# The second token tile's transposes move behind the high products of the first tile's second half unit, and TensorE's two layer loops are written out

## The chip, the cores and the metric

The kernel runs on one core of one Trainium2 chip. The metric is the device time of one execution in microseconds, as the median of several runs. Weights and inputs come from the device's memory (HBM), and 340 MB of them pass through the core's DMA queues in one execution.

## The reference, cut to what matters

Two transformer blocks of two layers each run one after the other on 256 tokens of width 1024. In the first block a layer is:

```
h = rmsnorm(x, g_pre_mix);  proj = h @ w_in;  four kinds of attention on slices of proj
x = x + rmsnorm(mix @ w_out, g_post_mix)
h = rmsnorm(x, g_pre_mlp);  m = square(relu(h @ w_up)) @ w_down;  x = x + rmsnorm(m, g_post_mlp)
x = x + sigmoid(x @ w_ple_gate) * (p_i @ w_ple_proj)
```

and in the second block:

```
z = x @ w_in + b_in;  dilated window attention and retention on slices of z;  gates;  mix = merged @ w_out
x = layer_norm(ALPHA * x + mix)
ffn = (silu(x @ w_gate) * (x @ w_up)) @ w_down;  x = layer_norm(ALPHA * x + ffn)
```

Everything is float32. The change touches the places where a new stage begins with a product of the freshly updated `x` and a weight matrix.

## The kernel before, in words

**Splitting.** Each float32 product is made of three products of shorter operands: high weights times high activations (`whi`, `XH`), high weights times low activations (`whi`, `XL`), and low weights times high activations (`wlo`, `XH`). The first two are called the high products here, the third the low products. ScalarE (ACT) makes the high part by a copy into the shorter type, and VectorE (DVE) makes the low part by a subtraction.

**Units.** A weight unit is 512 rows (four blocks of 128) by 512 columns, 1 MB. SyncE (SP) loads units into four slots of `raw`. ACT turns unit u into `whi[u % 2]` (line 1090, tile `whi`) and DVE turns it into `wlo[u % 2]` (line 1544, or in two halves at line 1556). The 256 tokens are two tiles m = 0 and m = 1 of 128. A half unit is a unit's work for one token tile: eight high products (lines 596 and 597, in turn), then four low products (line 602). A chunk of 512 output columns takes two units k = 0 and k = 1, so four half units, called m0k0, m0k1, m1k0 and m1k1 below.

**Turning.** Products contract over the 1024 features, so `x` must be transposed first. TensorE (PE) turns four 128 x 128 blocks into one of two banks of `T` (line 634), ACT copies the bank to `XH` (line 1090, times a gain vector in the first block's norms, then as four instructions of 128 columns), and DVE makes `XL` from it (line 1585 with the gain, line 1582 without), which also frees the bank. A token tile takes two banks, so eight transposes.

**A stage's beginning.** `first_chunk` is used at five places in a pair of layers, so at ten in the program: the first projection of a layer of the first block, its MLP (`U_MLP`), its PLE gate (`U_PLE1 + 1`), the first projection of a layer of the second block, and its feed-forward (`V_FFN`). Tile 0 has been turned before it, inside the last half unit of the stage ahead (`turn_ahead` as the `between` of `last_pair`). Then come m0k0, the turn of tile 1 (`row_turn`, which waits for `s_x`, set when DVE has written the new rows of `X` for tile 1), m0k1, m1k0 and m1k1. The rows of `X` come at line 1748 in the first block's norms and at line 2129 in the second block's.

**What sets the order.** Every engine's instructions are written out by hand in its own block, and each engine takes them strictly in that order. Semaphores (`s_hi`: `whi` ready, `s_lo`: `wlo` ready, `s_used`: unit consumed, `s_t`: bank turned, `s_thi`: `XH` ready, `s_tfree`: `XL` ready and bank free, `s_x` and `s_xh`: rows of `X` ready) tie them together. At the MLP's and the PLE gate's beginning ACT makes `whi` of unit k = 1 only after the square root that tile 1's norm needs, and DVE makes `wlo` of k = 1 between the new rows of `X` and tile 1's `XL`:

```
root(0, L, 4, 2, 1, 1)                    # ACT: square root of tile 1's norm
hi(0, L, 0, U_MLP + 1)                    # ACT: whi of unit k = 1
row_hi(0, L, T_N2, 1, pre[:, 1, L])       # ACT: XH of tile 1
...
add_normed(2, 1)                          # DVE: rows of X, tile 1
lo(0, L, 0, U_MLP + 1)                    # DVE: wlo of unit k = 1
row_los(0, L, T_N2, 1, pre[:, 1, L])      # DVE: XL of tile 1
```

At the feed-forward's beginning (`V_FFN`) and at a layer's beginning `whi` of k = 1 is ahead of that square root, or there is no norm. At the beginning of the program, and of layer 1 of the first block, ACT also squares `X` after tile 1's `XH`, for the norm's factor, and only then makes `whi` of unit 2.

**Layer loops.** ACT, DVE and GpSimd have their layers written out. TensorE and SyncE run each block's two layers in a hardware loop (`Fori`), so on TensorE the value that a semaphore is waited for is worked out from the loop's register by a register instruction.

## Time and profile before

| | |
|---|---|
| runs | 1994.34, 2001.11, 2001.44 us, median 2001.11 |
| the profiled execution's own time | 1996.49 us |
| its span, from first to last instruction | 1994.7 us |
| TensorE matmuls, busy | 1905.3 us, 96% of the span, 9135 instructions |
| VectorE, busy | 1172.4 us, 59% |
| ScalarE, busy | 887.9 us, 45% |
| mean granted TensorE clock | 0.976 of full speed |
| moved by DMA | 340.25 MB, 171 GB/s |

The span is what the rows' times count in. The execution's own time is 1.8 us more than it. An engine's busy time is the union of its instructions. PEld is TensorE's loading of weights, which runs beside its matmuls. Matmuls overlap in these rows: one of 512 columns lasts 0.39 us from start to end, and the next starts some 0.23 us after it.

### The profile page before, as it was taken

The page shows a single profiled execution, that of the slowest core. Times are in us where ns is not written, and L with a number is a line of the kernel's source. Part 1 is how long each engine was busy: PE and PEld are TensorE (multiplying, and loading weights), DVE is VectorE, ACT ScalarE, POOL GpSimd, SP SyncE. Part 2 cuts the span into 40 slices and gives each one's busy share as a digit, 9 for nine tenths or more (in the row PEclk, how much of TensorE's full clock was granted, in tenths as well). Part 3 has the DMA queues.
Part 4 walks back from the last instruction along what each step waited for, and adds up shares of the span by engine and source line. Part 5 has one row for each costly group of instructions (what it writes and reads, how often), then busy time and mean ns, then how long its engine had stood idle before and what let it go on. Part 6 is the DMA issues. An engine that isn't in the chain of part 4 may idle for free.

```text
span 1994.7 us, 25098 instructions
## 1 busy us (share of the span) xinstructions
PE 1905.3 (96%) x9135; PEld 1564.7 (78%) x9135; DVE 1172.4 (59%) x1372; ACT 887.9 (45%) x1071; POOL 82.3 (4%) x97
## 2 busy tenths in 40 slices
PE   7988999999899999999999989998999999989997
PEld 6777888778678887888877778886888877778885
DVE  5775555667765456556566565445556566574445
ACT  5544444555344445444345334443344355434442
POOL 5300000022100000000000000000000000000000
PEclk9989999999799999999999999999999999999998
DMA  7404555553755555664455644555663455645553
GB/s 260 141 15 154 189 183 166 177 190 113 86 190 195 182 174 181 216 213 124 143 189 173 224 152 160 186 184 190 213 215 122 147 185 191 209 149 164 186 186 106
DMA packets 194402, 340.25 MB, mean 171 GB/s; under 512 B 9338, under 2 KB 59418, under 8 KB 194316
## 3 DMA queue, kind: packets, MB, share of 16 engines
q1 hardware_dynamic: 189072, 327.76, 50.0%
q0 software_dynamic: 5120, 11.15, 3.1%
q8 instruction: 60, 0.98, 0.2%
q10 hardware_dynamic: 123, 0.14, 0.0%
q14 instruction: 27, 0.21, 0.0%
HBM read 333.24 MB, written 5.77 MB: 170 GB/s over the span
## 4 chain that ended last, share of the span: by engine, by line
PE 83%; DVE 8%; ACT 3%; DVEq 3%; issue 2%; DMA 1%; SPq 0%; ACTq 0%
PE G L580 18%; PE G L581 18%; PE G L585 18%; PE T L634 5%; PE A L580 4%; PE A L581 4%; PE A L585 4%; PE G L602 2%; PE G L596 2%; PE G L597 2%; DVE wlo L1544 2%; ACT whi L1090 2%; PE T L684 1%; PE A L694 1%; ACT arena L1090 1%
## 5 line engine op out<-in xcount | busy, mean ns | idle before, releaser
L1544 DVE TENSOR_TENSOR wlo<-raw,whi 128x2048 fp32r<-128x2048 f32 (+2 forms) x316 | 666.7, 2111 | 617.9 <-ACT whi L1090 617.4
L1090 ACT ACTIVATE whi<-raw 128x2048 fp32r<-128x2048 f32 (+3 forms) x320 | 566.0, 1769 | 647.1 <-PE G L585 523.8
L580 PE MATMUL G<-whi,XH 128*128 128x512 f32 (+1 forms) x1408 | 560.8, 398 | 8.3 <-DVE XL L1568 6.6
L581 PE MATMUL G<-whi,XL 128*128 128x512 f32 (+1 forms) x1408 | 550.3, 391 | 0.0
L585 PE MATMUL G<-wlo,XH 128*128 128x512 f32 (+1 forms) x1408 | 346.2, 388 | 0.0
L580 PEld LDWEIGHTS G<-whi,XH 128*128 128x128 f32 x1408 | 266.7, 189 | 64.8 <-issue 8.4
L581 PEld LDWEIGHTS G<-whi,XL 128*128 128x128 f32 x1408 | 266.7, 189 | 54.1 <-issue 1.9
L585 PEld LDWEIGHTS G<-wlo,XH 128*128 128x128 f32 x1408 | 263.9, 188 | 53.6
L634 PE MATMUL T<-ident,arena 128*128 128x128 f32 x812 | 120.7, 289 | 25.5 <-ACT arena L1090 18.1
L634 PEld LDWEIGHTS T<-ident,arena 128*128 128x128 f32 x812 | 99.3, 148 | 45.3 <-ACT arena L1090 15.3
L1090 ACT ACTIVATE arena<-T 128x512 f32<-128x512 f32 (+2 forms) x92 | 46.2, 550 | 151.2 <-PE T L634 150.9
L596 PE MATMUL G<-whi,XH 128*128 128x512 f32 x192 | 77.6, 404 | 7.9 <-ACT whi L1090 6.4
L580 PE MATMUL G<-whi,MH 128*128 128x512 f32 x216 | 84.4, 391 | 0.0
L581 PE MATMUL G<-whi,ML 128*128 128x512 f32 x216 | 84.1, 389 | 0.0
L597 PE MATMUL G<-whi,XL 128*128 128x512 f32 x192 | 76.6, 399 | 0.0
L580 PE MATMUL A<-whi,MH 128*128 128x512 f32 x192 | 74.7, 389 | 0.0
L581 PE MATMUL A<-whi,ML 128*128 128x512 f32 x192 | 74.7, 389 | 0.0
L580 PE MATMUL A<-whi,XH 128*128 128x512 f32 (+1 forms) x160 | 62.2, 390 | 0.0
L581 PE MATMUL A<-whi,XL 128*128 128x512 f32 (+1 forms) x160 | 60.4, 379 | 0.0
L1090 ACT ACT_TABLE_LOAD x40 | 51.3, 1283 | 9.3 <-PE T L634 8.6
L585 PE MATMUL G<-wlo,MH 128*128 128x512 f32 x216 | 55.1, 389 | 0.0
L602 PE MATMUL G<-wlo,XH 128*128 128x512 f32 x192 | 54.3, 405 | 0.7 <-DVE wlo L1544 0.5
(225 smaller groups left out, 2066.7 us busy)
## 6 DMA issues: line engine op xcount, KB each, us to landing
raw<-in_w_in SPq DMA_DIRECT2D x112, 1024.0 KB, 6.7
raw<-in_w_mlp_up SPq DMA_DIRECT2D x32, 1024.0 KB, 5.4
raw<-in_w_mlp_down SPq DMA_DIRECT2D x32, 1024.0 KB, 5.0
raw<-in_w_ffn_gate SPq DMA_DIRECT2D x44, 512.0 KB, 4.0
raw<-in_w_ffn_up SPq DMA_DIRECT2D x44, 512.0 KB, 5.0
raw<-in_w_ffn_down SPq DMA_DIRECT2D x44, 512.0 KB, 3.3
raw<-in_w_out SPq DMA_DIRECT2D x16, 1024.0 KB, 5.0
raw<-in_w_ret_proj SPq DMA_DIRECT2D x16, 1024.0 KB, 5.1
```

Of the source, the lines that this page charges most:

```text
L580: nc.tensor.matmul(dst(m), hx[:, k0 + k, rows], hi[:, k, :], start=first and k == 0, stop=False)
L581: nc.tensor.matmul(dst(m), lx[:, k0 + k, rows], hi[:, k, :], start=False, stop=False)
L585: mm = nc.tensor.matmul(dst(m), hx[:, k0 + k, m * P:(m + 1) * P], lo[:, k, :], start=False, stop=last and k == kb - 1)
L596: nc.tensor.matmul(dst(m), hx[:, k0 + k, rows], hi[:, k, :], start=first and k == 0, stop=False)
L597: nc.tensor.matmul(dst(m), lx[:, k0 + k, rows], hi[:, k, :], start=False, stop=False)
L602: mm = nc.tensor.matmul(dst(m), hx[:, k0 + k, rows], lo[:, k, :], start=False, stop=last and k == kb - 1)
L634: tr = nc.tensor.transpose(T[:, t % 2, n * P:(n + 1) * P], src, ident[:])
L684: mm = nc.tensor.matmul(heads_out(q)[:, h * HD:(h + 1) * HD], PT2[m][:, h, kt, g * P:(g + 1) * P], ZV[:, kt, (g * HG + 2 * x + h) * HD:][: ...
L694: mm = nc.tensor.matmul(A[:, q % 2, u * HD:(u + 1) * HD], PT[:, q % 2, kt, u * P:(u + 1) * P], Z[:, kt, col:col + HD], start=kt == 0, stop ...
L1090: return nc.scalar.activation(out_, in_, func, **kw)
L1544: tt(wlo[:, c % PARTS, 0:n], raw[:, slot, 0:n], whi[:, c % PARTS, 0:n].bitcast(F32), ALU.subtract).then_inc(s_lo.sem, 1)
```

## The change

`row_turn` for tile 1 is no longer issued ahead of m0k1. It goes into m0k1 as its `between`, so between that half unit's eight high products and its four low products. And both layer loops of TensorE become Python loops, so that its instructions for the two layers stand one behind the other in the program. The loops inside a layer (over the MLP's and the feed-forward's column groups) stay hardware loops. No other engine's code is changed.

```diff
                 for m in range(TILES):
                     for k in range(2):
-                        if (m, k) == (0, 1):
-                            row_turn(blk, L, t, 1, s_x, x)
                         pe.wait_ge(s_tfree.sem, s_tfree.at(blk, L, t + 2 * m + k + 1))
-                        half_unit(blk, L, m, c + k, XH, XL, UK * k, UK, bank_pair(group), k == 0, k == 1)
+                        half_unit(blk, L, m, c + k, XH, XL, UK * k, UK, bank_pair(group), k == 0, k == 1,
+                                  between=(lambda: row_turn(blk, L, t, 1, s_x, x)) if (m, k) == (0, 1) else None)
...
-            with pe.Fori(0, DEPTH) as L:
+            for L in range(DEPTH):
 
                 first_chunk(0, L, 0, 0, 0)
...
-            with pe.Fori(0, DEPTH) as L:
+            for L in range(DEPTH):
                 def w_in_chunk(i, c, u):
```

On TensorE, at the beginning of the first block's MLP, the turn of tile 1 (`T<-ident,X`) stands before the change between m0k0's low products and m0k1's high products:

```order
L602 MATMUL A<-wlo,XH 128x512 [waits s_lo]
L602 MATMUL A<-wlo,XH 128x512 x3
L634 MATMUL T<-ident,X 128x128 [waits s_tfree,s_x]
L634 MATMUL T<-ident,X 128x128 x3
L632 REGISTER_ALU [waits s_x]
L634 MATMUL T<-ident,X 128x128 [waits s_tfree]
L634 MATMUL T<-ident,X 128x128 x3
L596 MATMUL A<-whi,XH 128x512 [waits s_hi,s_tfree]
L597 MATMUL A<-whi,XL 128x512
```

and with the change, at the same place, the last high products of m0k1 are ahead of it and its low products behind it:

```order
L596 MATMUL A<-whi,XH 128x512
L597 MATMUL A<-whi,XL 128x512
L634 MATMUL T<-ident,X 128x128 [waits s_tfree,s_x]
L634 MATMUL T<-ident,X 128x128 x3
L634 MATMUL T<-ident,X 128x128 [waits s_tfree,s_x]
L634 MATMUL T<-ident,X 128x128 x3
L602 MATMUL A<-wlo,XH 128x512 [waits s_lo]
L602 MATMUL A<-wlo,XH 128x512 x3
L596 MATMUL A<-whi,XH 128x512 [waits s_hi,s_tfree]
L597 MATMUL A<-whi,XL 128x512
```

The transposes have moved past eight matmuls and past the wait for `whi` of unit k = 1 (`s_hi`), and what parts them from m1k0, the first half unit that needs their result, is now four matmuls where it was twelve.

At the end of a layer of the second block TensorE has, before the change, a register instruction and a taken branch behind the last low products (`A<-wlo,MH`):

```order
L602 MATMUL A<-wlo,MH 128x512 [waits s_lo]
L602 MATMUL A<-wlo,MH 128x512
L933 REGISTER_ALU
L933 COMPARE_AND_BRANCH
L174 UNCONDITIONAL_BRANCH
```

and with the change the next layer's first half unit stands right behind them:

```order
L602 MATMUL A<-wlo,MH 128x512 [waits s_lo]
L602 MATMUL A<-wlo,MH 128x512
L596 MATMUL G<-whi,XH 128x512 [waits s_hi,s_tfree]
L597 MATMUL G<-whi,XL 128x512
L596 MATMUL G<-whi,XH 128x512
L597 MATMUL G<-whi,XL 128x512
```

The branch and its register instruction are gone. Of the 300 register instructions in TensorE's program before the change 40 are left.

## Rows read from the trace of the kernel before

**Rows 1.** The page, chain that ended last, by engine

```profile
PE 83%; DVE 8%; ACT 3%; DVEq 3%; issue 2%; DMA 1%; SPq 0%; ACTq 0%
```

**Rows 2.** Timeline, MLP's beginning, layer 0: start, us, engine, operation [idle before]

```profile
186.97 1.08 PE L602 MATMUL A<-wlo,XH 128*128 128x512 f32 x4
188.74 1.90 ACT L1090 ACTIVATE whi<-raw 128x2048 fp32r<-128x2048 f32 x1
189.91 1.39 PE L634 MATMUL T<-ident,X 128*128 128x128 f32 x8 [1.86 <-DVE X L1748]
194.05 0.50 PE L596 MATMUL A<-whi,XH 128*128 128x512 f32 x1
```

**Rows 3.** Timeline, turn of tile 0: with the gain (182 us), without it (373 us)

```profile
182.00 1.03 PE L634 MATMUL T<-ident,X 128*128 128x128 f32 x8
...
185.00 0.50 PE L596 MATMUL A<-whi,XH 128*128 128x512 f32 x1 [1.03 <-DVE XL L1585]
...
372.97 1.03 PE L634 MATMUL T<-ident,X 128*128 128x128 f32 x8
...
374.24 1.29 DVE L1582 TENSOR_TENSOR XL<-T,XH 128x512 fp32r<-128x512 f32 x2 [0.24 <-ACT XH L1090]
```

**Rows 4.** Timeline, beginning of the PLE gate, layer 0

```profile
383.77 0.47 PE L596 MATMUL G<-whi,XH 128*128 128x512 f32 x1 [0.39 <-ACT whi L1090]
...
387.06 0.40 PE L596 MATMUL G<-whi,XH 128*128 128x512 f32 x1
```

**Rows 5.** Timeline, beginning of the program

```profile
18.95 1.03 PE L634 MATMUL T<-ident,X 128*128 128x128 f32 x8
...
25.58 1.92 ACT L1090 ACTIVATE whi<-raw 128x2048 fp32r<-128x2048 f32 x1 [0.23 <-DVE stat L1607]
...
28.01 0.39 PE L580 MATMUL G<-whi,XH 128*128 128x512 f32 x1
```

**Rows 6.** Timeline, beginning of layer 1 of the first block

```profile
408.64 1.34 PE L634 MATMUL T<-ident,X 128*128 128x128 f32 x8
...
412.58 0.41 PE L596 MATMUL G<-whi,XH 128*128 128x512 f32 x1
...
414.45 1.07 PE L602 MATMUL G<-wlo,XH 128*128 128x512 f32 x4
...
418.07 0.39 PE L580 MATMUL G<-whi,XH 128*128 128x512 f32 x1
```

**Rows 7.** Timeline, beginning of the second block

```profile
800.86 1.04 PE L634 MATMUL T<-ident,X 128*128 128x128 f32 x8
...
804.50 0.39 PE L596 MATMUL G<-whi,XH 128*128 128x512 f32 x1
```

**Rows 8.** Timeline, beginning of the feed-forward, layer 0 of the second block

```profile
1195.30 1.79 PE L634 MATMUL T<-ident,X 128*128 128x128 f32 x8 [3.52 <-DVE X L2129]
...
1195.83 2.29 DVE L1544 TENSOR_TENSOR wlo<-raw,whi 128x2048 fp32r<-128x2048 f32 x1
...
1200.90 0.39 PE L596 MATMUL A<-whi,XH 128*128 128x512 f32 x1
```

**Rows 9.** Timeline, beginning of layer 1 of the second block

```profile
1390.80 0.67 DVE L1582 TENSOR_TENSOR XL<-T,XH 128x512 fp32r<-128x512 f32 x1
...
1393.49 0.49 PE L596 MATMUL G<-whi,XH 128*128 128x512 f32 x1 [2.79 <-ACT whi L1090]
...
1398.95 2.28 DVE L1544 TENSOR_TENSOR wlo<-raw,whi 128x2048 fp32r<-128x2048 f32 x1
...
1402.41 0.39 PE L596 MATMUL G<-whi,XH 128*128 128x512 f32 x1
```

**Rows 10.** Timeline, m0k0 of the MLP's beginning in layer 1 of the first block

```profile
577.96 0.51 PE L596 MATMUL A<-whi,XH 128*128 128x512 f32 x1 [2.25 <-DVE XL L1585]
...
581.26 1.32 PE L602 MATMUL A<-wlo,XH 128*128 128x512 f32 x4
```

**Rows 11.** Windows of that stretch: engines' busy us, PEclk the granted clock

```profile
578.40:581.60 3.20, 3.20 (x9) 2.52 (x8) 3.09 (x9) 0.43 (x3) 0.00 (x0) 0.50 0.41 116
```

## The prediction

> **What bounds the kernel now.** I read the page first: TensorE holds 83% of the chain that ended last, the rest is mostly VectorE [rows 1]. So nearly every microsecond in which TensorE idles or starts late is on the path, and the change is worth what it does to TensorE's idle time at the ten beginnings of a stage. Then I read the timeline around each of them, with one question: when does m1k0 start, the first half unit that needs tile 1, and what let it start? Three patterns come out.
>
> At the MLP's beginning TensorE ends m0k0 at 188.05, idles 1.86 us for the rows of `X`, turns tile 1 at 189.91, and starts m1k0 at 194.05 [rows 2]. The idle 1.86 us look like the room for m0k1's eight high products. But these need `whi` of unit 1, which ScalarE makes from 188.74 to 190.64 [rows 2]: at 188.05 there is nothing that they could run on. The PLE gate is the same: today TensorE even waits 0.39 us for that `whi`, and starts the high products at 383.77 [rows 4].
>
> At the beginning of the program, of layer 1 of the first block and of the second block there is no long wait for `X`: the turn starts at once [rows 5 to 7].
>
> At the feed-forward's beginning, and at layer 1 of the second block, `whi` is early and `X` late: 3.52 us idle ahead of the turn in the first of them [rows 8]. Here there is something to fill.
>
> **The change part by part.** Prices first. Eight high products take 414.45 - 412.58 = 1.87 us [rows 6]. From the start of a turn to the start of the half unit that needs it are 185.00 - 182.00 = 3.00 us with a gain; without it the first half of `XL` is there at 374.24 + 0.65, so 1.92 us after 372.97, and I take 2.0 [rows 3]. ScalarE and VectorE do that work, and TensorE's products no longer cover it: of twelve matmuls four are left between, 0.9 us.
>
> MLP's beginning, two layers: the high products start when `whi` is there, 190.7, and end at 192.55. Only then comes the turn, and m1k0 at 195.55 instead of 194.05: +1.5 us each, +3.0. Queued behind the wait for `whi` is now the turn itself, and behind the turn ScalarE's `XH` and VectorE's `XL`; that is where the stall goes.
>
> PLE gate, two layers: 383.77 + 1.87 + 2.0 = 387.64 against 387.06 [rows 4]: +0.6 each, +1.2.
>
> Beginning of the program: the turn moves from 18.95 to 20.82. Behind it ScalarE squares `X` and takes the root, and only then makes `whi` of unit 2, which now ends at 27.50, so 8.55 us after the turn's start; it would end at 29.37, and unit 2 start at 29.4 instead of 28.01 [rows 5]: +1.4. Layer 1 of the first block: the turn from 408.64 to 410.51, m1k0 from 412.58 to 413.5, and unit 2, by the same 8.55, from 418.07 to 419.1 [rows 6]: +1.0.
>
> Second block's beginning: 800.86 + 1.87 + 2.0 = 804.73 against 804.50 [rows 7]: +0.2. These five terms make +6.8.
>
> Feed-forward, two layers: the high products fill idle time and are done before `X` comes. m0k1's low products then wait for `wlo`, which ends at 1195.83 + 2.29 = 1198.12 [rows 8]; they take 1.0, so m1k0 starts at 1199.15 instead of 1200.90: -1.7 each, -3.4. What is late next is VectorE, which makes `wlo` behind the rows of `X`. Layer 1 of the second block: `wlo` ends at 1401.23, m1k0 starts at 1402.25 instead of 1402.41 [rows 9]: -0.15.
>
> The clock. After the 2.25 us idle ahead of 577.96 the granted clock is 0.50 (1.2 GHz) [rows 10, 11], and eight high products take 581.26 - 577.96 = 3.30 us, 1.4 more than at 2.4 GHz. The change moves idle time: at the feed-forward it turns one long wait into two with only the transposes between (3.52 - 1.87 = 1.65 us, then some 1.4 for `wlo`), so I leave a fall there, 1.2 each, and the two beginnings give -1.0 together. At layer 1 of the second block I take half a fall, with the -0.15: +0.5. At the MLP of layer 0 the idle time grows from 1.86 to 2.6 us, and at the PLE gate it becomes one stretch of 2.8 us, where now the transposes divide it. Nothing (no fall) and 1.4 each are the bounds for these three, and since 2.25 us was enough for a fall once I take +2.0 for all.
>
> The layer loops. 260 of 300 register instructions go. Sixteen matmuls across three changes of semaphore take 418.07 - 414.45 = 3.62 us, 0.226 each, less than the 0.234 inside a half unit [rows 6]. So TensorE's sequencer works them out ahead, under running matmuls, and where matmuls run they are worth nothing. Without that cover (a wait that ends TensorE's idle time) they would cost a few hundredths each; bounds 0 and 0.1 us at each of the ten beginnings, and I take -0.3.
>
> The taken branch at the end of a layer does show: `XL`'s first half is written at 1390.80 + 0.67 = 1391.47, `whi` long before, and TensorE starts at 1393.49 [rows 9]. 2.0 us are lost there. But the way to m1k0 is VectorE's, which works without a gap to the rows of `X` and then `wlo` at 1398.95; an m0k0 that starts 2 us sooner waits there. So in the sum the branch is worth no more than the 0.15 above. The Trainium skill (Runtime: NRT & Kernel Launch, Instruction fetch mechanics) says that a taken branch whose target is not in the sequencer's window must fetch its page before execution goes on, and that kernels therefore do better written out. The 2.0 us in the row agree; by the page alone the two branches would give back some 4 us, and the sum would be that much lower.
>
> Sum: 6.8 - 1.0 + 0.5 + 2.0 - 0.3 = +8.0 us, 0.4%. On the profiled execution's own 1996.5 that is 2004.5. The median of the runs shown is 4.6 above that execution, so +8.0 on it is 2009.1. The three runs lie at 1994, 2001 and 2001; I forecast 2007, between the two.
>
> **The rivals.** (a) Faster: the loops pay. The mechanism is the register instruction ahead of a wait; the place, every wait of the layers. If each of the 260 that go freed 0.07 us, that is 18 us, and with +8.0 the kernel is 10 us faster, 1991; below that price it isn't faster by 0.5%. For it: the branch's 2.0 us. Against it: 0.226 us per matmul across three of them [rows 6]. 7%.
>
> (b) The move hardly bites: the products that no longer cover the turn were covering waits that come anyway, or the following stages give the 6.8 back, with only the feed-forward's -3.4 and the loops' -0.3 left: some -4 to +2 us, 1997 to 2003. For it: VectorE's work sets m1k0 at the MLP too. Against it: TensorE is 83% of the chain [rows 1] and unit 2's `whi` comes late as well [rows 5], so little there swallows a delay. 14%.
>
> (c) The clock falls at more beginnings than I count, and longer: 1.4 at each of MLP, gate, feed-forward and layer 1, twice where it falls for two stretches. +6 to +9 over the 6.8, so +13 to +16: 2014 to 2017. For it: 2.25 us of idle time sufficed. Against it: 1.86 us did not [rows 2], where the products behind it kept their 0.23 us. 25%.
>
> **How the numbers follow.** The forecast, +4 to +12 us, has 54%: its own range is 2001 to 2013. The 8 in 10 reach from 1997 (b's end) to 2016 (nearly c's end). 0.5%, 10 us, is about what a measurement of this kernel tells from no change. Above it lie all of (c) and a sixth of the forecast's cases: 0.34. Below lies (a): 0.07. Between: 0.59.
>
> **What would show it.** Right: at the MLP's beginning the first transposes of tile 1 stand 1.9 us behind the end of `whi`, and m1k0 starts 7.5 us after m0k0's end where it is 6.0 now; TensorE idle for `XL` ahead of m1k0 at the MLP, gate, program and layer beginnings, near 1 us each, where today there is none; at the feed-forward m1k0 starts some 1.1 us behind `wlo` rather than 2.8; unit 2 after the program's beginning starts right at the end of its `whi`. Wrong: transposes at the MLP's beginning as soon as `X` is there; pitches of unbroken products below 0.226 us; no idle time ahead of m1k0. The prediction fails low if the loops' instructions were on the path, and high if rows of products at 0.43 us each stand at most of these beginnings.

## The result, and the profile after the change

The changed kernel takes 2003.6 us (median of 11 runs, 1999.8 to 2009.71), the kernel before 1997.25 us (median of 11 runs beside them, 1994.34 to 2001.44). The ratio is 1.0028, 95% interval 1.0015 to 1.0041: 5.6 us slower. The forecast was 2007 and +8.0 us.

Part of the spread within a kernel goes with the mean granted clock of a run. The changed kernel's fastest run has 1999.8 us at 0.979, its slowest 2009.71 us at 0.971: 1.2 us for 0.001. A least-squares fit over all runs of this study, with one level for each kernel, gives 1.17 us. (Of a run of 2000 us, 0.001 of mean clock is 2 us at full speed that are missing, so not all of what the clock takes is on the path.) Below, "at equal clock" is the mean of a kernel's runs, each brought to a clock of 0.975 with this slope: before 1997.3, after 2003.7. Most of these figures are good to about 0.5 us, e5's to 0.7 and e9's to 1.1. It takes out what a kernel wins or loses through the clock, so it is no measure of a change that works on the clock.

The page of the profiled run (2004.16 us, span 2002.4), busy time by engine and the chain that ended last:

```profile
span 2002.4 us, 24552 instructions
...
PE 1910.1 (95%) x9135; PEld 1568.6 (78%) x9135; DVE 1174.2 (59%) x1372; ACT 888.1 (44%) x1071; POOL 78.8 (4%) x97
...
PE 82%; DVE 8%; ACT 3%; DVEq 3%; issue 2%; DMA 1%; SPq 0%; ACTq 0%
```

The page hardly tells the two kernels apart [rows 1]: TensorE is busy for 4.8 us more with the same 9135 matmuls, so more of them ran at half clock, and the other 2.9 us of the span are idle time. The change is seen only at the stage beginnings. Timeline of the changed kernel, MLP's beginning in layer 0, TensorE and `whi` of unit 1 (in this kernel lines behind the edit have numbers one lower):

```profile
187.88 0.50 PE L596 MATMUL A<-whi,XH 128*128 128x512 f32 x1 [1.03 <-DVE XL L1584]
189.84 1.08 PE L602 MATMUL A<-wlo,XH 128*128 128x512 f32 x4
...
191.63 1.89 ACT L1089 ACTIVATE whi<-raw 128x2048 fp32r<-128x2048 f32 x1
...
193.67 0.47 PE L596 MATMUL A<-whi,XH 128*128 128x512 f32 x1 [2.75 <-ACT whi L1089]
...
195.57 1.03 PE L634 MATMUL T<-ident,X 128*128 128x128 f32 x8
196.37 1.17 PE L602 MATMUL A<-wlo,XH 128*128 128x512 f32 x4
198.57 0.50 PE L596 MATMUL A<-whi,XH 128*128 128x512 f32 x1 [1.04 <-DVE XL L1584]
```

Against [rows 2]: TensorE's wait is no longer the 1.86 us for `X` but 2.75 us for `whi`; the turn starts 2.05 us behind the end of that `whi`; the four low products don't cover `XH` and `XL`, and 1.04 us of idle time stand ahead of m1k0.

The same chunk at the feed-forward, layer 0, TensorE and VectorE:

```profile
1202.84 1.42 DVE L2128 SCALAR_TENSOR_TENSOR X<-X,stat,gains 128x512 f32<-128x512 f32 x2
1203.64 1.32 PE L634 MATMUL T<-ident,X 128*128 128x128 f32 x8 [1.68 <-DVE X L2128]
1204.17 2.29 DVE L1543 TENSOR_TENSOR wlo<-raw,whi 128x2048 fp32r<-128x2048 f32 x1
...
1206.51 2.08 PE L602 MATMUL A<-wlo,XH 128*128 128x512 f32 x4 [1.55 <-DVE wlo L1543]
1208.38 0.63 PE L596 MATMUL A<-whi,XH 128*128 128x512 f32 x1
```

and windows of the changed kernel in the PLE gate of layer 1 and at the two feed-forwards (span of the window, busy us of PE, PEld, DVE, ACT and POOL, granted clock, DMA share, GB/s):

```profile
786.20:789.40 3.20, 3.20 (x13) 2.80 (x12) 1.17 (x2) 0.67 (x2) 0.00 (x0) 0.50 0.31 70
1206.20:1209.20 3.00, 2.69 (x6) 2.16 (x7) 1.45 (x3) 0.00 (x0) 0.00 (x0) 0.50 0.50 151
...
1800.60:1806.00 5.40, 5.11 (x12) 4.05 (x13) 1.43 (x3) 0.00 (x0) 0.00 (x0) 0.50 0.33 97
```

The high products now fill idle time, as foreseen: the 3.52 us ahead of the turn [rows 8] became 1.68, with 1.55 us more behind it. But the granted clock is 0.50 (1.2 GHz) when the low products start, and half-speed products (0.63 us each where 0.39 is full speed) follow.

**The account by place.** Every kernel here has the same matmuls (throwaway ones aside), so stretches can be compared by the start of two matmuls. Below, in us, from the start of tile 0's turn to the start of m1k0, and, behind the slash, to the first matmul behind m1k1 (at the program's beginning, where the first loads vary, from m0k0's first product):

| beginning | before | after | difference |
|---|---|---|---|
| program | 8.59 / 14.03 | 9.07 / 14.77 | +0.5 / +0.7 |
| MLP, layer 0 | 12.05 / 17.65 | 13.68 / 19.31 | +1.6 / +1.7 |
| PLE gate, layer 0 | 14.08 / 19.56 | 14.75 / 20.31 | +0.7 / +0.8 |
| layer 1, first block | 9.87 / 15.36 | 10.69 / 16.39 | +0.8 / +1.0 |
| MLP, layer 1 | 13.28 / 18.84 | 14.82 / 20.44 | +1.5 / +1.6 |
| PLE gate, layer 1 | 14.08 / 19.56 | 16.13 / 21.60 | +2.1 / +2.0 |
| second block | 8.84 / 14.28 | 8.95 / 14.52 | +0.1 / +0.2 |
| feed-forward, layer 0 | 15.07 / 20.51 | 14.29 / 20.22 | -0.8 / -0.3 |
| layer 1, second block | 13.42 / 18.86 | 13.43 / 18.90 | 0.0 / 0.0 |
| feed-forward, layer 1 | 14.78 / 20.22 | 14.29 / 21.62 | -0.5 / +1.4 |

The beginnings give +9.2 us. What lies between them gives -1.5: the first matmul of the program starts 1.0 us later (it waits for a load, and lies between 6.8 and 8.3 us in the fourteen profiles), the way from the second block's beginning to each feed-forward is 2.2 us shorter (375.89 to 373.73, and 375.95 to 373.77), and the other ways differ with their half-clock stretches: +1.1 ahead of the MLP of layer 0, +1.6 behind the last beginning, -1.2 ahead of layer 1 of the second block, +0.2 elsewhere. The spans differ by 7.7.

Two rows of the table need a warning. The profile of the kernel before happens to have no half-clock stretch in the MLP of layer 0. Five kernels that don't move the turn there (e1, e3, e6, e8, e11) have one and take 18.64 to 18.79 us for the chunk, e5, e10 and e12 have none and take 17.40 or 17.41. So a profile of another execution could have shown +0.6 where this one shows +1.7. And +1.4 of the +2.0 at the gate of layer 1 are a fall of the clock.

### The profile page after: what moved, and what is told of

Same layout as the page of the kernel before. It is cut to its first block, busy times and chain, and to the rows that moved or that the text cites. A ratio compares the mean times of both kernels' runs of the same rounds, so it can differ in the third digit from the quotient of the medians.

```text
span 2002.4 us, 24552 instructions
## 1 busy us (share of the span) xinstructions
PE 1910.1 (95%) x9135; PEld 1568.6 (78%) x9135; DVE 1174.2 (59%) x1372; ACT 888.1 (44%) x1071; POOL 78.8 (4%) x97
## 4 chain that ended last, share of the span: by engine, by line
PE 82%; DVE 8%; ACT 3%; DVEq 3%; issue 2%; DMA 1%; SPq 0%; ACTq 0%
PE G L580 18%; PE G L581 18%; PE G L585 18%; PE T L634 4%; PE A L580 4%; PE A L585 4%; PE A L581 4%; PE G L596 2%; PE G L597 2%; PE G L602 2%; DVE wlo L1543 2%; ACT whi L1089 2%; PE T L683 1%; PE A L693 1%; ACT arena L1089 1%
## 5 line engine op out<-in xcount | busy, mean ns | idle before, releaser
L580 PEld LDWEIGHTS G<-whi,XH 128*128 128x128 f32 x1408 | 266.0, 189 | 64.5 <-DVE XL L1567 7.9
L596 PEld LDWEIGHTS G<-whi,XH 128*128 128x128 f32 x192 | 37.3, 195 | 26.3 <-DVE XL L1584 8.6
```

Of the source, the lines that this page charges most:

```text
L580: nc.tensor.matmul(dst(m), hx[:, k0 + k, rows], hi[:, k, :], start=first and k == 0, stop=False)
L596: nc.tensor.matmul(dst(m), hx[:, k0 + k, rows], hi[:, k, :], start=first and k == 0, stop=False)
```

## The experiments

Twelve kernels. Ratios are to runs of the kernel before on the same chip; e1 to e4, e5 to e8, e9 to e11 and e12 ran on four different chips, so between these groups the ratios compare better than the medians.

| run | median us | ratio (95%) | at equal clock |
|---|---|---|---|
| before (78 runs beside e1 to e12) | 1997.0 | | 1997.3 |
| after | 2003.6 | 1.0028 (1.0015 to 1.0041) | 2003.7 |
| e1, loops only | 2000.16 | 1.0014 (1.0004 to 1.0025) | 1997.9 |
| e2, move only | 2002.99 | 1.0036 (1.0022 to 1.0050) | 2004.3 |
| e3, move where `X` is late | 1996.29 | 0.9997 (0.9983 to 1.0011) | 1997.1 |
| e4, after with early `whi` | 1995.98 | 0.9995 (0.9984 to 1.0006) | 1997.0 |
| e5, before with early `whi` | 1994.12 | 0.9985 (0.9975 to 0.9995) | 1994.1 |
| e6, e3 with early `whi` | 1993.9 | 0.9981 (0.9971 to 0.9991) | 1993.2 |
| e7, not at two starts | 2005.82 (one run) | | 2002.3 |
| e8, e6 with idle time filled | 1991.48 | 0.9966 (0.9953 to 0.9979) | 1993.9 |
| e9, no cover | 2027.05 | 1.0148 (1.0132 to 1.0165) | 2021.9 |
| e10, unmoved, filled | 1989.57 | 0.9954 (0.9941 to 0.9967) | 1992.4 |
| e11, e8 and more filled | 1989.28 | 0.9950 (0.9937 to 0.9962) | 1993.7 |
| e12, e10 with hardware loops | 1993.84 | 0.9987 (0.9978 to 0.9997) | 1994.7 |

### e1 and e2: the two halves of the change

e1 is the kernel before with the first edit alone, e2 with the second:

```
e1  -            with pe.Fori(0, DEPTH) as L:        (both blocks)
    +            for L in range(DEPTH):
e2  -                        if (m, k) == (0, 1):
    -                            row_turn(blk, L, t, 1, s_x, x)
    +                        half_unit(..., between=(lambda: row_turn(blk, L, t, 1, s_x, x)) if (m, k) == (0, 1) else None)
```

> The kernel before with TensorE's two layer loops written out and nothing moved. My theory: no change in time that can be told (0 to -2 us against the kernel before). The 2.8 us of idle time ahead of layer 1 of the second block shrink to about 0.6 us (some 2 us of branch are gone), but m1k0 there, which waits for VectorE, comes at most 0.2 us sooner; where matmuls run without a gap nothing changes. Rival 1, register instructions are on the path: 0.07 us for each of 260 makes it 10 us or more faster. Rival 2, the two taken branches are fully on the path, 2 us each: -4 us. The Trainium skill (Runtime: NRT & Kernel Launch, Instruction fetch mechanics) would have it by rival 2.

> The kernel before with only the turn of tile 1 moved behind the high products of m0k1; both layer loops stay hardware loops. My theory: the move makes all of the change, so this run is as the changed kernel, 4 to 8 us slower than the kernel before, with about 1 us of idle time for XL ahead of m1k0 at the MLP and the program's beginning. Layer 1 of the second block keeps its 2.8 us of idle time and loses only what the half-clock stretch there costs. Rival (the loops written out gave some microseconds back in the changed kernel): this run is 4 us or more slower than the changed kernel, so 10 us slower than before.

The move makes the whole loss (e2, 1.0036), and the written-out loops gain nothing: e1 is 0.14% slower where 0 to 2 us faster was expected, and equal at equal clock (0.6 us more, with an error as large). Its timeline at the beginning of layer 1 of the second block:

```profile
1391.02 1.93 PE L634 MATMUL T<-ident,X 128*128 128x128 f32 x8 [3.42 <-DVE X L2129]
1392.60 1.20 PE L602 MATMUL A<-wlo,MH 128*128 128x512 f32 x2
...
1395.98 1.09 PE L602 MATMUL G<-wlo,XH 128*128 128x512 f32 x4
1400.53 1.68 PE L634 MATMUL T<-ident,X 128*128 128x128 f32 x8 [3.46 <-DVE X L2129]
```

and in the kernel before, at the same turn:

```profile
1398.42 1.39 PE L634 MATMUL T<-ident,X 128*128 128x128 f32 x8 [0.34 <-DVE X L2129]
```

The 2.79 us ahead of m0k0 [rows 9] are gone, with the branch in them; the next wait grew from 0.34 to 3.46 us instead. (In the kernel before most of m0k0 also ran at half clock, which hid in the same wait.) From tile 0's turn to tile 1's it is 9.43 us before and 9.51 in e1: VectorE's rows of `X` set it in both. The Trainium skill (Runtime: NRT & Kernel Launch, Instruction fetch mechanics) says that a taken branch whose target is outside the sequencer's window must first fetch its page. The trace agrees that there is a stall, 2.0 us with the branch and 0.06 us without it, from the `XL` that m0k0 needs to its start, though not that the fetch is its cause. It was not on the path.

At the feed-forward, where nothing but the loop differs, e1 is 0.9 us longer to m1k0 in layer 0 and 1.2 in layer 1 (15.98 and 15.95). Windows of e1 and, below it, of the kernel before, some 3 us behind the turn in each (turns at 1197.50 and 1195.30):

```profile
1200.00:1203.00 3.00, 3.00 (x8) 2.32 (x8) 1.50 (x3) 0.10 (x1) 0.00 (x0) 0.50 0.45 151
```

```profile
1196.30:1199.30 3.00, 3.00 (x10) 2.52 (x9) 3.00 (x3) 0.89 (x2) 0.00 (x0) 0.50 0.00 0
...
1200.00:1203.00 3.00, 3.00 (x15) 2.47 (x14) 0.00 (x0) 0.00 (x0) 0.00 (x0) 1.00 0.39 145
```

Behind 3.5 us of idle time both run at 0.50, and e1 stays there longer. Why isn't settled. The same goes for the MLP of layer 0, where e1's chunk is 1.0 us longer with a fall that the kernel before doesn't have.

What the loops do win lies elsewhere. First products of a unit in the second block, kernel before and kernel after:

```profile
1117.91 0.47 PE L580 MATMUL G<-whi,XH 128*128 128x512 f32 x1 [1.91 <-DVE XL L1568]
```

```profile
1126.21 0.50 PE L580 MATMUL G<-whi,XH 128*128 128x512 f32 x1 [1.72 <-DVE XL L1567]
```

The same wait, 0.19 us shorter without the register instruction. Four more such waits of a layer are 0.07 to 0.19 shorter, 0.65 us in all with this one, while four short waits of 0.25 us are 0.09 longer, most of which the products behind them give back. The other part is the clock: on the way from the second block's beginning to its first feed-forward (375.9 us with hardware loops, in all four profiles; 373.7 to 373.8 written out, in eight of ten, 375.3 and 375.4 in e9 and e11) a half-clock stretch stands wherever it is long. On the same way in layer 1 e2 and e5 have 374.4 and 374.2 us with none, against 373.7 to 373.9 written out, which leaves 0.4 to 0.7 us for the register instructions. A stretch costs 1.6 us there. Six of the eight ways with hardware loops have one and two of the twenty written out; why, no run shows. The stretch of the kernel before:

```profile
940.20:943.20 3.00, 3.00 (x11) 2.61 (x11) 2.52 (x4) 2.29 (x4) 0.00 (x0) 0.50 0.18 66
```

### e3, e7 and e9: where the move costs, and what

e3 moves the turn only where `X` comes late; e7 leaves out the first block's two layer starts:

```
e3  +  inside = blk == 1 and (L, c) != (0, 0)     # else row_turn ahead of m0k1, as before
e7  +  inside = (blk, c) != (0, 0)
e9  +  if (m, k) == (1, 0):                       # all ten: a step further back
    +      row_turn(blk, L, t, 1, s_x, x)
```

> Loops written out; the turn of tile 1 is moved only at the feed-forward (both layers) and at layer 1 of the second block, where the high products can run while the rows of X are still being made; at the other seven beginnings it stands ahead of m0k1 as before. My theory: feed-forward -2.0 us each at full clock, +1.2 to +2.9 for the half-clock stretch behind it, layer 1 of the second block -2 and +1.8: in all -3 to 0 us against the kernel before, and 6 us faster than the changed kernel. Rival (the moved turns at the MLP, gate and starts are hidden, and what the changed kernel lost it lost through the clock at the feed-forward): this run is as the changed kernel, 4 to 8 us slower than before.

> The changed kernel, with the turn ahead of m0k1 as before at the beginning of the program and of layer 1 of the first block, moved elsewhere. My theory, by the trace: no idle time for XL ahead of m1k0 at these two places (1.04 and 0.73 us in the changed kernel), unit 2 of the program's beginning about 1.4 us sooner and of layer 1 about 1.0 us, counted from the first transposes of the program, all of it kept until the MLP: 2.4 us faster than the changed kernel. Rival (the delay of the starts is taken up again by waits for ScalarE and VectorE further on): the distance from the first product to the MLP of layer 0 is as in the changed kernel.

> The changed kernel with the turn of tile 1 a step further back at all ten beginnings: behind m0k1's low products, right ahead of m1k0, so that no product covers ScalarE's XH and VectorE's XL. My theory (what the move costs is the cover, 0.23 us for each matmul that no longer lies between turn and m1k0): four matmuls less, so m1k0 0.9 to 1.0 us later than in the changed kernel at the MLP, the gate and the three starts (7 places), and about 2 to 3 us later at the feed-forward and layer 1 of the second block, where the turn now stands behind the wait for wlo too: 12 to 16 us slower than the changed kernel, idle time for XL ahead of m1k0 of 2 us with the gain, 1 us or more without it. Rival (VectorE's and ScalarE's queues set m1k0, whichever place the turn has): within 3 us of the changed kernel.

e3 takes back the whole loss (0.9997): it was made at the MLP, the gates and the starts, not at the feed-forward. What the feed-forward wins is little. (e3's MLP of layer 0, with the turn not moved, is one of those with a fall, 18.69 us, so there it is only 0.6 us shorter than the changed kernel's.)

e7 shows at the two starts what was expected: no idle time ahead of m1k0, layer 1 9.82 us to m1k0 as before (after: 10.69). Its one time is no answer: the mean clock was 0.972, and half-clock stretches lay in both gates (16.28 and 17.29 us to m1k0). By place the delay is kept: from m0k0's end to the MLP of layer 0 the changed kernel takes 165.6 us and e7 164.1, with 30.8 us at half clock on that way in both, so its rival fails.

e9 costs 1.2% over the changed kernel, some 23 us by the medians, 18 at equal clock and 19.6 by the profiled spans: more than the 12 to 16 of the theory, and far beyond the rival. Its layer 1 of the first block:

```profile
417.73 2.29 DVE L1544 TENSOR_TENSOR wlo<-raw,whi 128x2048 fp32r<-128x2048 f32 x1
...
420.07 1.22 PE L602 MATMUL G<-wlo,XH 128*128 128x512 f32 x4 [0.88 <-DVE wlo L1544]
421.13 1.03 PE L634 MATMUL T<-ident,X 128*128 128x128 f32 x8
424.12 0.50 PE L596 MATMUL G<-whi,XH 128*128 128x512 f32 x1 [1.96 <-DVE XL L1585]
```

From turn to m1k0 it is 2.99 us, as in [rows 3] and as in the changed kernel (3.00), and the idle time in it has grown from 0.73 us there to 1.96: with four matmuls fewer as cover, that is the price of the cover. I had missed the 0.88 us above it: the turn had also filled the wait for `wlo`, which now comes on top; at the feed-forward that wait is 4.52 us. At the MLP of layer 1 e9's wait for a load is 4.6 us longer, but the way to it is 4.8 us shorter, so that this adds nothing to its time (last section).

### e4, e5 and e6: `whi` ahead of the square root

```
MLP   -  root(0, L, 4, 2, 1, 1)
         hi(0, L, 0, U_MLP + 1)
      +  root(0, L, 4, 2, 1, 1)
gate  +  hi(0, L, 0, U_PLE1 + 2)
         root(0, L, 7, 4, 1, 1)                   # e4: on after, e5: on before, e6: on e3
         ... copy of the projection ...
      -  hi(0, L, 0, U_PLE1 + 2)
```

> The changed kernel, and ScalarE makes whi of unit k = 1 ahead of the square root of tile 1's norm at the MLP's and the PLE gate's beginning (and ahead of the copy of the projection there), four places in all; no other engine is changed. My theory: what the move costs there is the wait for that whi, since the turn is queued behind it. With whi early the high products of m0k1 run in the idle time, the turn starts when X is there, and m1k0 comes some 1.5 to 2 us sooner at the MLP (by VectorE's chain of wlo and XL, about where the kernel before had it) and 0.6 to 1 us at the gate; the idle time of 2.7 us ahead of m0k1 is gone at all four. In all 3 to 6 us faster than the changed kernel, so within 2 us of the kernel before. Rival (m1k0 there is set by VectorE's wlo and XL, whichever way the turn lies, and a later square root delays the rows of X by as much as whi takes, 1.9 us): no gain against the changed kernel, or a loss of up to 4 us.

> The kernel before (nothing moved, hardware loops) with ScalarE's whi of unit k = 1 made ahead of the square root of tile 1's norm at the MLP and the PLE gate, as in the run with the move. My theory: at the MLP nothing, since m1k0 there waits for VectorE's XL behind wlo of k = 1 and not for ScalarE; at the gate the 0.39 us wait for whi goes and up to 1 us each is won. In all 0 to -2 us against the kernel before: the early whi is worth 4 to 7 us only where the turn is queued behind it. Rival (the early whi is an improvement of its own, whichever way the turn lies): 4 us or more faster than before, and then the moved turn is no better covered by it than the unmoved one.

> Loops written out, the move only where the rows of X are late (feed-forward in both layers, layer 1 of the second block), and the early whi at the MLP and the gate. My theory: the sum of the parts, -2 us at each feed-forward less its half-clock stretch, -1 us at each gate: 1 to 4 us faster than before, 7 to 10 us faster than the changed kernel. Rival (what VectorE's chain allows is used up already, and the clock takes back the rest): within 1 us of the kernel before.

e4 is 0.33% faster than the changed kernel (7.6 us by the medians, 6.6 at equal clock), a little more than expected, and that is all of the changed kernel's loss. But the places are not alike. Its MLP's beginning in layer 0:

```profile
188.41 1.98 ACT L1089 ACTIVATE whi<-raw 128x2048 fp32r<-128x2048 f32 x1
...
192.54 1.32 PE L634 MATMUL T<-ident,X 128*128 128x128 f32 x8
195.40 1.90 PE L602 MATMUL A<-wlo,XH 128*128 128x512 f32 x4 [1.55 <-DVE wlo L1543]
```

The 2.75 us for `whi` are gone, and the turn follows the rows of `X` at once. But now VectorE's `wlo` is late, 1.55 us, and the clock falls behind it: to m1k0 it is 12.48 us, of the 1.6 lost only 1.2 are back, and at the end of the chunk 0.4. At the MLP of layer 1 nothing comes back: from the start of its first `whi` to the chunk's end e4 takes 20.4 us, the changed kernel 20.6, before and e5 18.9. There 10.2 us run at half clock in e4, over m0k0 and into m0k1, where the changed kernel has 3.4, and the turn, queued behind eight high products more, still leaves 1.04 us idle for `XL`. At the gates all comes back and more: 12.94 us in layer 0, against 14.75 after and 14.08 before, and 12.93 in layer 1 against 16.13. So it is at the gates that the wait for `whi` was the whole loss; at the MLP it is a part, and the move costs there even with `whi` early.

The surplus at the gates doesn't need the move: e5 has 13.03 and 13.04 at the gates, 11.90 at the MLP of layer 0, and is 3.0 us faster than before, more than the 0 to 2 of its theory and less than the 4 of its rival. So early `whi` and move each have their own account: 3 us for the one by itself, and 3 to 4 more of it only to undo the other. e6 joins the good parts, 3.8 us faster than before, though no more than 1 us of it beyond e5.

### e8, e10, e11 and e12: the clock, taken out

```
e8   in m0k1 of both feed-forwards and of layer 1, second block:
     +  for _ in range(11): nc.tensor.transpose(T[:, (t + 2) % 2, 0:P], ident[:], ident[:])
        row_turn(blk, L, t, 1, s_x, x)
     +  for _ in range(10): nc.tensor.transpose(other[:, 1, 0:P], ident[:], ident[:])
e10  ahead of the unmoved turn, at the same three places: range(24) of the first
e11  e8, and range(24) ahead of the turn at the end of the second block's layers
e12  e10 with hardware loops, and without the filling at layer 1
```

> As the run with late X and early whi, and the two idle stretches of m0k1 at the feed-forward (both layers) and at layer 1 of the second block are filled with throwaway transposes of the identity: 11 ahead of the wait for X, 10 behind the turn, ahead of the wait for wlo. Their results are overwritten or not read. My theory: the clock falls there because TensorE idles; filled, the granted clock stays at 1.00 through m1k0, where the run without them has 0.50 to 0.75, and 1.2 to 2 us are kept at each of the three places, 3 to 6 us in all. Rival 1 (throwaway transposes don't keep the clock): the half-clock stretches stand as they are and the time is the same. Rival 2 (they run past the moment when X or wlo is ready): up to 0.5 us lost at each place, so up to 1.5 us slower.

> Loops written out, early whi, and nothing moved: the turn of tile 1 is ahead of m0k1 at all ten beginnings. The idle time ahead of it at the feed-forward (both layers) and at layer 1 of the second block is filled with 24 throwaway transposes of the identity, whose results are overwritten. It stands against the run with the turn moved at these three places and its idle time filled. My theory: what the move wins at the feed-forward is mostly the clock, since at full clock eight high products (1.87 us) fit between the turn and the moment when wlo is ready (1198.12, against 1195.30 + 1.0 + 1.9 = 1198.2), so this run has the same time within 1.5 us, with m1k0 at most 0.3 us later at each of the three places. Rival (the products that run ahead of the turn are won whatever the clock): 1.7 us slower at each place, 5 us in all.

> As the run with moved turns, early whi and filled idle time, and 24 more throwaway transposes ahead of the wait for X at the end of each layer of the second block (3.3 us idle in the changed kernel). My theory: the granted clock stays at 1.00 there too; in layer 0 the four low products and the start of layer 1 run at full clock, which wins 1 to 2 us; layer 1's end has only the program's tail behind it, 0 to 1 us. In all 1 to 3 us faster than without them. Rival (VectorE sets the next stage's beginning, so a faster clock only lengthens the wait): no change within 1 us.

> The kernel before with the early whi and the 24 throwaway transposes ahead of the turn at the feed-forward (both layers), and both layer loops kept as hardware loops: the run with nothing moved and its idle time filled, but for the loops (and for the filling at layer 1 of the second block). It tells what the written-out loops are worth once the clock does not take it back. My theory: 3 to 5 us slower than that run. Of it 1.3 us are register instructions ahead of waits that end idle time (five waits of a layer of the second block, 0.07 to 0.19 us each), 1.7 us one half-clock stretch between the beginning and the feed-forward of the second block, which all three profiles with hardware loops have and none of those written out, and up to 1.5 us the unfilled beginning of layer 1. The 2 us of the branch are hidden by VectorE. Rival 1 (the loops written out are worth nothing): the same time within 1 us. Rival 2 (branch and register instructions are on the path): 6 us or more slower.

e8's feed-forward in layer 0, timeline and two windows:

```profile
1194.47 1.36 PE L663 MATMUL T<-ident 128*128 128x128 f32 x11
...
1196.33 1.32 PE L634 MATMUL T<-ident,X 128*128 128x128 f32 x8 [0.50 <-DVE X L2140]
1197.49 1.26 PE L667 MATMUL G<-ident 128*128 128x128 f32 x10
1199.20 1.19 PE L602 MATMUL A<-wlo,XH 128*128 128x512 f32 x4 [0.45 <-DVE wlo L1555]
1200.23 0.40 PE L596 MATMUL A<-whi,XH 128*128 128x512 f32 x1
```

```profile
1196.30:1199.30 3.00, 2.51 (x19) 2.03 (x19) 3.00 (x3) 1.19 (x2) 0.00 (x0) 1.00 0.03 5
1199.30:1202.30 3.00, 3.00 (x14) 2.46 (x15) 1.04 (x2) 0.00 (x0) 0.00 (x0) 1.00 0.56 171
```

With TensorE kept at work the granted clock stays at 1.00, where e6 without the filling has this behind its turn at 1194.37:

```profile
1199.00:1202.00 3.00, 3.00 (x8) 2.33 (x8) 0.00 (x0) 0.00 (x0) 0.00 (x0) 0.50 0.44 159
```

The chunk takes 18.91 us to its end, against 21.67 in e6 (in layer 1, where e6's profile has no fall, both have 18.90). In time that is 2.4 us by the medians, under the 3 to 6 expected, with intervals that overlap; at equal clock e8 is no faster than e6, as it should be if the clock is all that it wins.

All profiles together say it more clearly. At the two feed-forwards half-clock products stand ahead of m1k0 in six of six cases with the turn unmoved and nothing filled (before, e1, e5), in nine of twelve with it moved and nothing filled (after, e2, e3, e4, e6, e7), and in none of eight where the idle time was filled (e8, e10, e11, e12).

e10 is the run that decides on the feed-forward term. Nothing is moved, the idle time is filled:

```profile
1188.38 2.78 PE L657 MATMUL T<-ident 128*128 128x128 f32 x24
...
1192.05 1.32 PE L634 MATMUL T<-ident,X 128*128 128x128 f32 x8 [0.89 <-DVE X L2131]
...
1195.06 1.09 PE L602 MATMUL A<-wlo,XH 128*128 128x512 f32 x4
...
1195.98 0.39 PE L596 MATMUL A<-whi,XH 128*128 128x512 f32 x1
```

From the turn to m1k0 it is 3.93 us; with the turn moved and filled (e8) it is 3.90, with the turn moved and unfilled 4.74, and in the kernel before 5.60 [rows 8]. Over the whole chunk e10 has 18.92, 18.88 and 18.89 us at the three places and e8 18.91, 18.86 and 18.90. At full clock the move wins 0.03 us at most. The three feed-forwards that were moved, unfilled and by chance kept the clock say the same. One of them is e2's in layer 0:

```profile
1203.17 1.32 PE L634 MATMUL T<-ident,X 128*128 128x128 f32 x8 [1.66 <-DVE X L2128]
1206.04 1.20 PE L602 MATMUL A<-wlo,XH 128*128 128x512 f32 x4 [1.54 <-DVE wlo L1543]
1207.07 0.39 PE L596 MATMUL A<-whi,XH 128*128 128x512 f32 x1
```

It too has 3.90 us from turn to m1k0, and the chunks of the three take 18.82 (e2), 18.88 (e3) and 18.90 us (e6). So without a fall the chunk takes 18.8 to 18.9 us, wherever the turn stands and whether or not the idle time is filled; with a fall it takes 20.2 to 21.7 (e9, whose turn stands further back, left out). All that the move seemed to win was a half-clock stretch made a little shorter.

By time e10 is 1.9 us faster than e8 by the medians and 1.5 at equal clock, so the move isn't worth anything there either. Its profile has no fall at the MLP of layer 0, and fewer half-clock stretches on the way to it; e8's has both.

e11 is no clear gain over e8: at layer 1 of the second block it has 18.90 us against 18.86, so VectorE sets that beginning, as its rival had it. e10 and e11 are the fastest of the study, 0.46% and 0.50% below the kernel before, and not to be told apart (their intervals reach into e8's).

e12 against e10 tells what the written-out loops are worth when nothing takes the clock back: 0.33% by the ratios, 4.3 us by the medians (of two chips), 2.3 at equal clock. By place: 2.15 and 2.09 us on the ways to the two feed-forwards, where it has 375.95 and 375.84 us, of which some 1.6 each are a half-clock stretch; 1.58 at the beginning of layer 1, which is the missing filling and not the loops; nothing at the feed-forwards (13.47 us to m1k0, e10 13.48 and 13.45). So the loops are worth about 4 us there, three quarters of it through the clock, and a single pair of profiles is behind it.

## Why the prediction was right, and where it was not

**Right by mechanism and size: the MLPs, the gates and the three starts (program, layer 1 of the first block, second block).** "The turn itself" queued behind the wait for `whi`: the trace shows it at both MLPs and both gates, and e4 shows that it is the whole loss at the gates and a part of it at the MLPs. The MLP's +1.5 each measured +1.6 and +1.5, the gate's +0.6 measured +0.7 (layer 0), layer 1's +1.0 the same, the second block's +0.2 measured +0.1 to m1k0 and +0.2 to the chunk's end. The program's +1.4 measured +0.7 for the chunk, but from m0k0's end to unit 2 it is 9.06 us before and 10.52 after, so the +1.4 is there; m0k0 itself, most of it at half clock, took 4.97 us before and 4.25 after, and it varies from 4.25 to 5.26 over the profiles.

Of the signs that I named, the turn 1.9 us behind `whi` (2.05), m1k0 7.5 us after m0k0's end (190.92 to 198.57, 7.65), and unit 2 of the program right behind its `whi` (29.82 against 29.68) stand in the trace. So does the idle time for `XL` ahead of m1k0 at the program's beginning (1.04), the MLPs (1.04 each) and layer 1 (0.73), but not at the gates and the second block, where it is 0.06 us or less: those turns have no gain vector to apply, and the four low products just cover ScalarE's and VectorE's work. At the feed-forward m1k0 starts 1.9 us behind `wlo`, not 1.1, since the products between run at half clock.

**Wrong: the feed-forward, "-1.7 each".** I read the 2.8 us from `wlo` to m1k0 in [rows 8] as the cost of the order. The first row of that group said otherwise: the turn itself lasted 1.79 us, where [rows 2], also behind idle time, has 1.39 and [rows 7] 1.04, so the clock was down, and m0k1 behind it ran at half speed. At full clock the turn and eight high products end 0.2 us behind `wlo` (e10: `wlo` is written at 1194.86, the low products start at 1195.06). e10 against e8 measures the move there at 0.03 us. What was left was the clock, and for it I took "+1.2 each" as something that the change adds, though it had been there. Term and correction together were -1.0; the trace has -0.3 and +1.4.

**Wrong: the loops, "-0.3".** The register instructions ahead of waits that end idle time cost 0.07 to 0.19 us, the branch nothing, as forecast. But there are ten such waits in the second block alone, 1.3 us less what eight short waits take back, so about 1 us. And each of the two ways to the feed-forwards had a half-clock stretch before and has none after, 1.6 us each. So -4.3 us between the beginnings in the profiled runs, not -0.3. In e1, too, the ways are 4.2 us shorter, and it gives that back, in rows at half clock: 0.9 and 1.2 at the feed-forwards and 1.6 at layer 1 of the second block, and 1.0 more at the MLP of layer 0. That the net is nothing was right, for a reason that I did not have.

**By size: the clock at the MLP of layer 0 and the gates, "+2.0 for all".** The trace has one fall, +1.4 at the gate of layer 1, and none at the other two places. Over the profiles of after, e2, e7 and e9, whose gates all wait 2.7 us for `whi`, six of eight gates had one. The size of one fall, 1.4 us, was right. **Layer 1 of the second block, "+0.5"**, is 0.0. The fall came, and longer (6.8 us at 0.50 where the kernel before has 3.4), but it lies over m0k0, which without the branch starts 2 us sooner and then waits for VectorE anyway.

**The sum.** Beginnings +8.3 forecast, +9.2 measured; the rest -0.3 against -1.5. The feed-forward came out 2.1 us above its term and the loops 4 us below theirs, and a late first load (+1.0) and stretches of half clock elsewhere made up the rest. That +8.0 and the +7.7 of the two profiled spans lie so close is partly luck, since errors of opposite sign cancelled. The 2007 also rests on a base of 1999, between the three times that I had; the median of eleven runs is 1997.25.

**The rivals.** (a), loops that pay 10 us: e1. (b), a move that hardly bites: e2 and e3. (c), more falls of the clock: it lives in part, the clock did fall at a gate and longer at a feed-forward, but the kernel before lost as much of it elsewhere (mean clock 0.975 over all runs, both before and after).

## What to carry to other kernels

Work that another engine continues should stand ahead of every wait that it doesn't need, and with as many independent products behind it as the other engines need time; price a move by the cover that it takes away and by the waits that the moved step had itself been covering. Before an idle stretch is booked as a gain, look at the duration of the rows behind it: where they are longer than elsewhere the clock is down, and a few throwaway transposes may win what the new order would, and more: the kernels with them and the turn left where it was are among the fastest here. A run's mean granted clock is worth 1.2 us for 0.001 here, so a change of 0.2% should be read from stretches between the same two instructions as well as from the time, and from more than one profile.

## What the runs showed of the hardware

- The granted clock can fall on idle time that is broken up. In the changed kernel 1.68 and 1.55 us of idle time with only eight transposes between them are followed by 0.50; in e8 the same stretches with 11 and 10 transposes in them by 1.00.
- Whether a given wait brings the fall is not fixed. The two broken stretches at a feed-forward did in nine of twelve cases; 2.7 us at the gate, over the four kernels whose gates have that wait (after, e2, e7, e9), in six of eight (four of four in layer 1, two of four in layer 0).
- Half-clock stretches weigh differently by place. On the way from the program's beginning to the MLP of layer 0 they grow together with the time, from 20.5 us at 0.50 and 152.9 us in all (e2) to 37.6 and 156.8 (e11), with the other twelve profiles in order between. Apart from the layer loop no edit of this study is on that way, so this is scatter of up to 4 us.
- On the same way in layer 1 it counts for nothing, because the MLP of layer 1 begins when its first weights land, in every profile. ScalarE waits 1.6 us for them in the changed kernel, 6.17 in e9 and 5.48 in e4, which arrived early. In e4:

```profile
577.69 1.91 ACT L1089 ACTIVATE whi<-raw 128x2048 fp32r<-128x2048 f32 x1 [5.48 <-DMA raw<-in_w_mlp_up]
```

  Counted from tile 0's turn at layer 1's beginning, that `whi` starts 170.8 to 171.6 us later in the ten profiles that leave the turn of tile 1 there unmoved, 172.1 to 172.3 in after, e2 and e4, and 174.5 in e9, while TensorE's own way to the MLP varies from 151.1 to 155.9 us. So up to 4 us that TensorE could be there sooner hang on this one load, issued behind two of gains and one of activations. No run here moved it; it is the next thing to try.
